# An encoder trunk on one core: order of the first units of both input projections, and what stands around the begin of each attention

## The reference

```
layer 0:  h = rms_norm(x);  proj = h @ w_in        (q, k, v of 8 dilated heads, latents of 8 more, a gate)
          y = concat(dilated window attention, latent attention) * silu(gate)
          x = x + rms_norm(y @ w_out)
layer 1:  the same frame around grouped-query attention: 16 query heads, 4 key heads,
          q and k normalised per head and rotated;  v, gate from the same projection
```

## Time and profile before

| | us |
|---|---|
| three runs | 2119.23, 2119.86, 2123.38 (median 2119.86) |
| profiled execution, its own time | 2123.5 |
| its span | 2121.7 |
| PE busy | 2045.0 (96%) |
| DVE, ACT, POOL busy | 1290.0, 1123.1, 951.9 |

### The profile page before, as it was taken

One profiled execution on the slowest core, in us unless ns is written; L12 is line 12 of the kernel. 1 busy time (PEld: TensorE's weight loads), 2 busy tenths in 40 slices (PEclk: granted clock), 3 DMA queues, 4 the chain that ended last, 5 costly groups with the idle time before them and its releaser, 6 DMA issues.

```text
span 2121.7 us, 25158 instructions
## 1 busy us (share of the span) xinstructions
PE 2045.0 (96%) x9334; PEld 1629.9 (77%) x9334; DVE 1290.0 (61%) x1922; ACT 1123.1 (53%) x1420; POOL 951.9 (45%) x477
## 2 busy tenths in 40 slices
PE   7999998999999999999997999999999999998997
PEld 5878886788888877777885777887777777775785
DVE  6232145325787667684668677524578877888554
ACT  7142234335666666665455444333577777777431
POOL 1222234334555565556001666523467667666501
PEclk9999999999999999999998999999999999999999
DMA  5133478527555554545335232261323333333434
GB/s 189 46 128 131 150 258 310 144 72 152 121 120 111 123 127 92 115 137 182 103 110 180 85 118 101 100 191 65 83 59 81 72 82 70 82 82 110 167 106 157
DMA packets 167578, 260.29 MB, mean 123 GB/s; under 512 B 75472, under 2 KB 84304, under 8 KB 167456
## 3 DMA queue, kind: packets, MB, share of 16 engines
q1 hardware_dynamic: 167456, 258.68, 42.5%
HBM read 160.72 MB, written 97.91 MB: 122 GB/s over the span
## 4 chain that ended last, share of the span: by engine, by line
PE 86%; DVE 8%; ACT 2%; issue 2%; DMA 1%; POOL 1%; SPq 0%; DVEq 0%; ACTq 0%
PE SA L1855 11%; PE OP L1899 9%; PE OP L481 5%; PE SA L481 5%; PE SM L1954 5%; PE OP L1006 5%; PE SA L1954 5%; PE SM L1781 5%; PE SA L1006 4%; PE OP L1906 4%; PE OS L481 3%; PE OS L1899 2%; PE OS L1006 2%; PE OS L1954 2%; PE SM L1777 2%
## 5 line engine op out<-in xcount | busy, mean ns | idle before, releaser
L2303 POOL TENSOR_TENSOR c_PL<-c_PF,c_PH 128x1024 fp32r<-128x1024 f32 x128 | 309.0, 2419 | 152.9 <-ACT c_PH L2031 81.7
L2303 POOL TENSOR_TENSOR ab_PL<-ab_PF,ab_PH 128x1024 fp32r<-128x1024 f32 (+3 forms) x128 | 266.5, 2085 | 190.3 <-ACT ab_PH L2031 130.7
L2028 ACT ACTIVATE ab_PF<-SA 128x1024 f32<-128x1024 f32 (+3 forms) x160 | 143.6, 897 | 159.9 <-PE SA L1816 86.8
L2108 DVE TENSOR_REDUCE c_MH<-SM 128x1 f32<-128x512 f32 x256 | 171.9, 687 | 76.7 <-PE SM L1781 76.2
L2028 ACT ACTIVATE c_PF<-SA 128x1024 f32<-128x1024 f32 x160 | 164.4, 1027 | 94.0 <-PE SA L1855 93.6
L402 POOL TENSOR_TENSOR e_wl<-e_raw,e_wh 128x1024 fp32r<-128x1024 f32 (+1 forms) x31 | 73.6, 2374 | 200.6 <-ACT e_wh L547 200.6
L2031 ACT ACTIVATE c_PH<-c_PF 128x1024 fp32r<-128x1024 f32 x128 | 135.8, 1061 | 4.1
L1855 PE MATMUL SA<-c_Q,c_KA 128*128 128x512 f32 x320 | 129.4, 404 | 8.7 <-ACT c_PF L2028 8.7
L1781 PE MATMUL SM<-c_KA,c_Q 128*128 128x512 f32 x320 | 127.3, 399 | 4.6 <-DVE c_MH L2108 3.2
L1855 PE MATMUL SA<-c_Q,c_KB 72*128 72x512 f32 x320 | 128.3, 401 | 0.0
L2099 DVE CUSTOM_DVE_ANT_0 ab_BS<-SM,ab_Bhi 128x512 f32<-128x512 f32 (+1 forms) x192 | 85.8, 464 | 62.6 <-PE SM L1777 62.4
(11 more groups left out here) (490 smaller groups left out, 6002.6 us busy)
## 6 DMA issues: line engine op xcount, KB each, us to landing
c_Q<-qC_hi SPq DMA_DIRECT2D x32, 384.0 KB, 4.9
e_raw<-in_w_tiles SPq DMA_DIRECT2D x20, 512.0 KB, 4.0
n_raw<-in_w_tiles SPq DMA_DIRECT2D x18, 512.0 KB, 3.7
e_XF<-in_xT SPq DMA_DIRECT2D x12, 512.0 KB, 10.3
silu_gate<-e_ta SPq DMA_DIRECT2D x24, 256.0 KB, 2.0
ab_Q<-qA_hi SPq DMA_DIRECT2D x16, 384.0 KB, 5.3
ab_G<-silu_gate SPq DMA_DIRECT2D x24, 256.0 KB, 3.2
ab_res<-in_xT SPq DMA_DIRECT2D x24, 256.0 KB, 2.9
```

What stands on the lines that cost most here:

```text
L2028: nc.scalar.activation(used(PF[p], h, s), used(SA, h, s), ACT.Exp).then_inc(e_done, 1)
L2108: nc.vector.reduce_max(dst, src, axis=AX_X).then_inc(m_done, 1)
L2303: nc.gpsimd.tensor_tensor(used(PL[p], h, s), used(PF[p], h, s), used(PH[p], h, s).bitcast(F32), ALU.subtract).then_inc(p_lo[0], 1)
```

## The change

In `entry`: ACT's squares get buffers of their own and don't wait for DVE; DVE makes all low parts first and adds only part of chunk 0's squares among them, the rest of chunks 0 and 1 in front of the first eviction, chunk 2's after unit 3. The second pair of x tiles is followed by the load of weights 1. PE takes units 0 to 5 in pairs, two tiles of one chunk together, each matmul as its operands come; the three sums stand inside the last pair and after units 6 and 8.

```diff
+    apart = [at(f"apart{i}", [P, CH], F32, REST + 18432 + 2048 * i) for i in range(9)]
+    x_squares = (apart[0:7], sh[0:4] + sl[0:3], ta + tb + apart[7:9])
+    x_total = (ssum[0], ssum[1], sl[3])
...
-        def load_x(c):
-            for k in range(0, KT, 2):
+        def load_x(c, k0=0, k1=KT):
+            for k in range(k0, k1, 2):
...
-        load_x(0)
+        load_x(0, 0, 4)
         load(1)
+        load_x(0, 4, KT)
...
+        def products_pair(n):
+
+            c = U[n][2]
+
+            def step(b, w, x, k, lo=False):
+                return nc.tensor.matmul(bank(n + b), w[b][:, k * P:(k + 1) * P], x[:, k, cols(c)],
+                                        start=(k == 0 and w is wh and not lo), stop=(lo and k == KT - 1))
+
+            def low(b, k):
+
+                pe.wait_ge(x_lo, c * KT + k + 1)
+                mm = step(b, wh, XL, k, True)
+                if k == KT - 1:
+                    mm.then_inc(mm_done, 1)
+
+            for i in range(KT + 4):
+                if i < KT:
+                    pe.wait_ge(x_hi, c * KT + i + 1)
+                    if n + i == 0:
+                        pe.wait_ge(w_hi, 1)
+                    step(0, wh, XH, i)
+                    if n + i == 0:
+                        pe.wait_ge(w_lo, 1)
+                    step(0, wl, XH, i)
+                if 1 <= i <= KT:
+                    if n + i == 1:
+                        pe.wait_ge(w_hi, 2)
+                    step(1, wh, XH, i - 1)
+                if i >= 4:
+                    if n + i == 4:
+                        pe.wait_ge(w_lo, 2)
+                    low(0, i - 4)
+                    if c < 2:
+                        step(1, wl, XH, i - 4)
+                        low(1, i - 4)
+            if c == 2:
+                x_square_sum(0)
+                for k in range(KT):
+                    step(1, wl, XH, k)
+                for k in range(KT):
+                    low(1, k)
...
+            if n < 6:
+                if n % 2 == 0:
+                    products_pair(n)
...
-            if n in (0, 2, 4):
-                x_square_sum(n // 2)
+            if n in (6, 8):
+                x_square_sum(n // 2 - 2)
...
+                if (c, k) == (0, 2):
+                    high_weights(1)
...
-                if k == 0:
-                    wait_count(act, total, c - 1)
-                else:
-                    wait_count(act, x_sum, (KT - 1) * c + max(0, k - 2))
-                out = ssum[c % 2] if k == 0 else sq[k % 2]
+                out = x_squares[c][k - 1] if k else x_total[c]
...
-        split_x(0)
-        high_weights(1)
-        split_x(1)
-        root(0, rstd[:, cols(0)], D)
-        split_x(2)
-        root(1, rstd[:, cols(1)], D)
+        for c in range(NC):
+            split_x(c)
         for n in range(N):
             for w in splits[n]:
                 high_weights(w)
+            if n in (5, 7, 9):
+                c = (n - 5) // 2
+                root(c, rstd[:, cols(c)], D)
             for m in (n, n - LAG):
...
+        for c in range(NC):
+            for k in range(KT):
+                low_x(c, k)
+                if c > 0 and k in (1, 4, 7):
+                    add_square(0, 3 * c - 2 + k // 3)
...
+            if n == 0:
+                add_square(0, KT - 1)
+                for k in range(1, KT):
+                    add_square(1, k)
```

```diff
-    U += [(tiles[t], t, c) for t in range(2, 12) for c in range(NC)]
+        ("values", u, 2, 512) for u in range(4)] + [("x", t, 8, D) for t in (12, 13, 14, 15, 16, 10, 17, 11)]
+    EARLY = 4
+    U = [(tiles[t], t, c) for c in ORDER[0:2] for t in range(2)]
+    U += [(tiles[2], 2, c) for c in ORDER] + [(tiles[t], t, c) for t in range(3, 12) for c in range(NC)]
     U += [(("value", i), V0 + 3, i) for i in range(TT // 2)]
-    U += [(late_gates[t], V0 + 4 + t, c) for t in range(6) for c in range(NC)]
+    for t in range(6):
+        if t == 5:
+            U += [(tiles[0], V0 + 9, ORDER[2])]
+        U += [(late_gates[t], V0 + 4 + t + t // 5, c) for c in range(NC)]
+    U += [(tiles[1], V0 + 11, ORDER[2])]
...
-    splits = [[w for w in range(2, len(W)) if max(first_unit[w - 1], last_unit[w - 2] + 1) == n] for n in range(N)]
+    splits = [[w for w in range(2, len(W)) if max(first_unit[w - 1], last_unit[w - 2] + 1 - (w > V0 + 5)) == n]
+              for n in range(N)]
...
+    def place_of(i):
+
+        return (i + 1) % 3
...
-        if (period, t) == (3, 0):
-            load(sp, 2)
+        if (period, t) in ((3, 0), (3, 1)):
+            load(sp, 2 + t)
...
-        for g in range(3):
-            gated(g)
-        low_weights(pool, 2)
-        for g in range(3, 6):
-            gated(g)
-        for n in range(6, N):
+        for g in range(EARLY):
+            gated(pool, g)
+        for n in range(EARLY, N):
+            if n == 6:
+                low_weights(pool, 4)
             for w in splits[n]:
-                low_weights(pool, w)
+                if w > 4:
+                    low_weights(pool, w)
             if n in qk:
                 rotate(n)
-            if n in gates:
-                gated(gates.index(n))
+            if n in gates and n < N - 1:
+                gated(pool, gates.index(n))
...
-        if w == 0:
+        if n in (0, 2, 6):
...
-            if i < 2:
-                pe.wait_ge(deviation, NC)
+            if i < 3:
+                pe.wait_ge(deviation, 3 - i % 2)
...
-            if n in (0, 2, 4):
-                x_square_sum(n // 2)
-            if n - 1 in qk and n != v0:
-                head_sums(n - 1)
+            if n in (0, 2, 7):
+                x_square_sum(min(n // 2, 2))
+            if n < v0:
+                for m in {8: (4, 5), 9: (6,), 10: (7,), 11: (8, 9), v0 - 1: (n - 2, n - 1)}.get(n, (n - 2,) if n > 11 else ()):
+                    head_sums(m)
...
+            if t in (4, 7):
+                high_weights(act, 2 + t // 7)
...
-        for g in range(3):
-            sigmoid(g)
-        high_weights(act, 2)
-        root(act, 2)
-        for g in range(3, 6):
-            sigmoid(g)
-        for n in range(6, N):
+        for g in range(EARLY):
+            sigmoid(act, g)
+        for n in range(EARLY, N):
+            if n == 5:
+                high_weights(act, 4)
+                root(act, 2)
...
+                for n in range(2):
+                    evict(dve, n)
...
-        dve.wait_ge(x_sum[1], KT - 1)
...
-            evict(n)
-            if n == 2:
-                for k in range(1, KT):
+            if n > 1:
+                evict(dve, n)
+            if n in (1, 2, 3):
+                for k in range(1, KT)[3 * (n - 1):3 * n]:
                     add_square(dve, 2, k)
+            if n == v0 - 1:
+                dve.wait_ge(tok_ready, 1)
+                nc.vector.tensor_copy(rtok[:], bank(v0 + 4)[:, 0:TT]).then_inc(tok_done, 1)
             if n - 1 in qk and n != v0:
                 finish(n - 1)
             if n - 2 in qk and n < v0:
                 low(n - 2)
-            if n in (4, 8):
-                prepare(n // 2 - 2)
-            if n == v0 - 1:
-                dve.wait_ge(tok_ready, 1)
-                nc.vector.tensor_copy(rtok[:], bank(v0 + 4)[:, 0:TT]).then_inc(tok_done, 1)
+            if n in (3, 8):
+                prepare(n // 4)
```

```diff
-                pe.wait_ge(late_set, 2)
+                pe.wait_ge(late_set, 3)
...
-            if g == MAX0 and part == 0:
-                pe.wait_ge(const_in, 16 * n_const)
-                pe.wait_ge(const_set, n_set)
             for u in units_beside(g)[part:part + 1]:
                 max_unit(0, u)
             if g in (sample_at, prompt_at) and part == 2:
+                pe.wait_ge(const_set, n_set)
...
+            if g == 3:
+                first.last_sigmoid(act)
...
-                set_ones(0, const_set)
-                nc.vector.memset(M[:].bitcast(F32), 0.0).then_inc(const_set, 1)
-                dve.wait_ge(const_set, n_set)
+                nc.vector.memset(M[:].bitcast(F32), 0.0).then_inc(late_set, 1)
+                dve.wait_ge(late_set, 1)
                 if NA:
                     bias(0, 0)
                     bias(0, 1)
-                    bias_full(0)
-                    bias(1, 0)
-                    bias(1, 1)
             for u in units_beside(g)[2:]:
                 maximum(0, u)
+            if g == MAX0:
+                set_ones(0, const_set, 0)
+                set_ones(0, const_set, 1)
+            if g == MAX0 and NA:
+                bias_full(0)
+            if g in (MAX0 + 1, MAX0 + 2) and NA:
+                bias(1, g - MAX0 - 1)
             if g == sample_at - 1 and NA:
                 both_sample(0)
             if g == prompt_at - 1:
...
-        set_ones(1, late_set)
...
+            if g in (6, 9):
+                set_ones(1, late_set, g // 9)
...
+            if g == 3:
+                first.last_gated(pool)
```

More of the change, by code:

```diff
@@ L156 @@
     gates_stored: Callable
+    last_sigmoid: Callable
+    last_gated: Callable
 @dataclass
```

(67 more changed lines are left out.)

111 lines of the change are left out of this document (35 added, 76 removed).

## The result

The changed kernel took **2109.3 us** (median of 5, 2107.3 to 2110.0) against 2119.9 before (median of 5 beside it, 2119.2 to 2123.4): ratio 0.9944, 95% interval 0.9932 to 0.9955. The profiled executions took 2123.5 and 2109.3, 14.2 apart. Forecast were 2088, a gain of 33.9 against the profile, and 2079 to 2101. It is faster, and the interval stays clear of 1, but the gain was a third of the forecast and the time lies outside the range.

A forecast was written before the change was run, and what follows sets the result against it. PE is busy 96% of the span, so only its idle or slow time can be won. Terms 3.0 + 6.4 + 1.5 + 3.3 + 3.0 + 16.7 = 33.9 off the profiled 2123.5 give 2089.6; forecast 2088, range 2079 to 2101.

The forecast's parts named there:

- part 3: Begin of each attention: first exponential no longer waits for last sigmoid, nor first maximum for ones; gains 3.3 and 3.0 us.
- the moved ones delay a maximum by up to 1.3, once a head: Attention: the only cost put on setting the ones later on VectorE, up to 1.3 us once a head.
- a queue of loads: Head 1's loads behind the last store; in a rival with other q-unit queues, 8 to 12 us more, 2098, chance 0.15.
- My sign of being wrong: PE in layer 1's first twelve units: a wait over 5 us, or many small ones for q and k.
- Part 1: First projection, first units in pairs so that ACT no longer waits for DVE: gain 3.0 us, bounds 1 and 4.5.
- Part 2: Constants: PE's waits at the max units of g = 7 go, gaining 6.4 us in layer 0 and 1.5 in layer 1.
- The cap by the loads: Layer 0's attention: head 1's loads wait for the last gate's product, so a gain of up to 5.8 is held to 3.3.
- the middle for the clock: Layer 1's attention begin: 4.3 us with the full clock, 1.8 if PE drops to 1.2 GHz; 3.0 taken.
- Part 4: Second projection, last third later, q units in front: PE's wait for the added squares goes, gain 16.7 us (11 to 18.7).
- The two terms that I put at 1 each: Second projection: weights 4 behind POOL's rotation, some 1 us; head sums wanting unit 9's square, 0 to 3.5, 1 taken.
- The rule of the Trainium skill: Two-input VectorE and SBUF-reading GpSimd instructions exclude each other; would make part 4's sum 2 us smaller.
- the profile's surplus over the median: Profiled 2123.5 against 2119.86: could be a low-clock stretch that part 3 already wins back; forecast set between 2089.6 and 2086.

The follow-up runs named there:

- e1: The changed kernel with the ones of the second VH set at g = 7 of the attention, not at g = 9: 2095.1 us, ratio 0.987.
- e10: e9 with ScalarE's head scale ahead of the square in units 6 to 10 of the second projection, and three adds behind evictions in the first: 2090.1 us.
- e5: The changed kernel run again without an edit: 2106.7 us, ratio 0.9935.
- e9: The changed kernel with the ones at g = 7 and the tables of k scaled after unit 20 of the second projection, not unit 8: 2093.3 us.
- e6: e1 with the ones of both second buffers set ahead of g = 0 again, as in the kernel before: 2099.3 us, ratio 0.9899.
- e7: e1 with the last sigmoid and gate product of both projections back at the end of the projection: 2100.5 us, ratio 0.9907.

## Why the prediction was wrong

**The step that failed** is the half sentence of part 3, "the moved ones delay a maximum by up to 1.3, once a head". It costed the moved memset by its length and by the maxima behind it, and didn't follow the semaphore that the diff changes in the same place, from 2 to 3. Who waits is PE, once in each layer, at g = 10, and what it waits for is all that DVE has queued ahead of the memset. That was 3.0 and 3.8 us, with the low clock 4.8 and 6.8; e1 gives back 10.7 of it. It is also no rival of mine: the rival for this place was a queue of loads (0 to 1.9 when measured). My sign of being wrong, a wait over 5 us or many small ones in the second projection, didn't come either (the longest there was 3.4), so it would have called the forecast right. With e1's edit the time is 2095.1, inside the range and 7 above the forecast.

The other terms, by the table of starts and the runs:

- Part 1, 3.0 forecast: 1.2 to 2.2 in the profiles with it, by the start of unit 12 (3.0 in e10). 0.2 was a wrong reading: 50.42 is the start of a piece of the chain, and PE began unit 6 at 50.26. The low clock lasted to 15.4, not 14, and unit 6 waited 0.43 (1.23 in e5, 0.97 in e9) for an eviction that stood behind adds which POOL's weight split held (three took 4.34). e10 without that wait has unit 6 at 45.5, where I had 45.7.
- Part 2, 6.4 and 1.5 forecast: 6.8 and 1.5. Right, and right in its reason.
- Part 3, the begins alone: 3.3 and 3.0 forecast, 5.05 and 5.5 measured. The mechanism was right (the gap in layer 0 went from 1.95 to 0.45, and the clock stayed at 1.00 in both). Layer 0 came within 0.8 of its bound of 5.8; layer 1 went 1.2 beyond its bound of 4.3, since its first steps took 2.3 to 2.4 and not the 2.79 that I had put in for all. The cap by the loads and the middle for the clock were both too careful.
- Part 4, 16.7 forecast: 11.4. Up to unit 6 of the second projection it gave 18.6 of 18.7. The two terms that I put at 1 each came as 0 at unit 9 (weights) and 3.4 at unit 11: the head sum, which waits for unit 9's square behind `prepare` and DVE's rounds of 5.6, at nearly its bound of 3.5. Behind it the clock fell (8.07 x 0.21 = 1.7 lost). 0.5 went to the weights that are loaded twice, which I had called hidden, and 1.7 to a fall at the token scales (10.11 x 0.17), which came in this profile and not in that of the kernel before nor in that of e5: 18.6 - 3.4 - 1.7 - 0.5 - 1.7 = 11.3.
- The rule of the Trainium skill ("SBUF — State Buffer", "Who interferes with whom") was to take 2 us in the low parts; there nothing was lost, PE had its sum at 1158.99 without a wait. But the traces agree with the rule in the catch-up, where DVE's multiplication took 1.04 or 1.66 with POOL's rotation beside it and 0.69 without, and so two rounds in e10 won nothing.
- The falls that come and go: 6.1 us outside the changed places in the first profile of the changed kernel (part of the 0.6 is waits), none of which I had; I had put the profile's surplus over the median the other way.

With the memset in its right place (e1) the change gives 26.6 against the 2121.7 of the kernel before beside it, so the one queue is 10.7 of the 19.7 that the profiles fell short of 33.9; the largest other terms are part 4 (5.3) and the falls (6.1), against which part 3 gave 4.3 more than forecast. With e10's edits it is 32.6 against 2122.7. That this comes near 33.9 is luck in part, since e10's three edits (tables, head scale, adds) weren't in the forecast.

## What to carry to other kernels

When a diff raises the number in a wait, find which instruction brings the last count, and price all that its queue holds ahead of it, not the instruction. A moved piece of work that is short and "anywhere" should stand at the earliest step where its engine is idle, not at the latest that seems safe. And an idle of some 2 us on PE can cost some 3 more by the clock (5.0 and 5.5 in all at the two begins of e6 and e7), so look for all causes of such a wait, here the ones in one layer and the sigmoid in the other. Before an order is swapped, as in e10, check what the instruction that now stands first waits for.

## What the runs showed of the hardware that I had not expected

- Behind idle stretches of 0.45, 0.70 and 1.03 at the begins the granted clock stayed at 1.00, behind 1.95 and 2.37 it fell each of eight times, to 1.2 GHz for part of the next 16 us (0.68 there in e6 and e7): one such wait cost 5.0 and 5.5 in all in these two. The length of the idle isn't all: behind 1.98 at g = 147 it fell in six profiles of twelve, and behind the 3.0 at head 1 of layer 0 in two of three.
- The row of one-column matmuls (3 us, PE busy) is a place where it falls too, in some executions: 1.00, 0.86 and 0.78 over the same two units behind it, and low in seven of the eleven profiles with the row whole. That the row is the cause isn't shown.
- A one-column product costs 0.24 in a row of its kind. A pair of them and one long matmul in turn take 0.99 at the full clock, 0.27 more than a pair in the row (0.49) and a long one in a full stream (0.227).
